# The address distance between the weight ring and the activation buffers in a two-layer decoder trunk

## What is computed

```python
h = x
for i in range(DEPTH):                      # DEPTH = 2
    xn = rmsnorm(h, g_mix[i])
    mix = attn_mixer(xn, ...) if i % 2 == 0 else rglru_mixer(xn, ...)
    h = h + mix
    h = h + swiglu(rmsnorm(h, g_ffn[i]), w_ffn_gate[i], w_ffn_up[i], w_ffn_down[i])
    gate = jax.nn.sigmoid(rmsnorm(h, g_ple[i]) @ w_ple_gate[i])
    h = h + gate * (p[i] @ w_ple_proj[i])   # p[i]: 256 tokens x 256
return rmsnorm(h, g_final)
```

## The kernel before

| tile | bytes from the ring's start | modulo 256 |
|---|---|---|
| w_hi, place s | 4224 s | 0, 128, 0, 128 |
| w_lo, place s | 16,896 + 4224 s | 0, 128, 0, 128 |
| pT_hi, pT_lo | 43,008 and 47,104 | 0 |
| xa_hi (a_off) | 56,640 | 64 |
| xa_lo, xb_hi, xb_lo, hid_hi | each 16,384 further | 64 |
| hid_lo | 45,056 behind hid_hi | 64 |

## Time and profile before

### The profile page before, as it was taken

How to read it: one execution, slowest core, us unless ns; L and a number is a source line. 1 busy time by engine, 2 the same in 40 slices (tenths; PEclk the granted TensorE clock), 3 DMA queues, 4 the chain that set the end, 5 groups by cost and what they waited for, 6 DMA issues and landing times.

```text
span 2471.5 us, 29756 instructions
## 1 busy us (share of the span) xinstructions
PE 2445.6 (99%) x11084; PEld 1994.7 (81%) x11084; DVE 1315.4 (53%) x1677; ACT 1139.5 (46%) x1533; POOL 3.2 (0%) x17
## 2 busy tenths in 40 slices
PE   8999999999999999999999999999999999999997
PEld 7888778888888888888888888888888888888886
DVE  5545665555454454444566676554454454444455
ACT  5435555544444444444454575544444444344454
POOL 0000000000000000000000000000000000000000
PEclk9999999999999999999999999999999999999999
DMA  7744435666666665555557445566666666555563
GB/s 215 229 120 120 131 117 182 185 187 186 187 187 182 186 186 184 187 188 187 187 187 235 140 154 178 186 183 185 187 187 184 186 183 188 186 187 187 187 204 135
DMA packets 234042, 443.87 MB, mean 180 GB/s; under 512 B 16184, under 2 KB 21344, under 8 KB 233824
## 3 DMA queue, kind: packets, MB, share of 16 engines
q1 hardware_dynamic: 233904, 442.62, 58.7%
q10 hardware_dynamic: 48, 0.02, 0.0%
HBM read 440.49 MB, written 2.10 MB: 179 GB/s over the span
## 4 chain that ended last, share of the span: by engine, by line
PE 96%; DVE 1%; ACT 1%; DMA 1%; issue 0%; ACTq 0%; DVEq 0%
PE ps L1278 30%; PE ps L1276 30%; PE ps L1277 30%; PE ps L1232 2%; PE ps L1487 1%; PE ps L1400 1%; PE ps L1331 1%; DMA raw<-in_w_in_rec_dram 1%; DVE w_lo L774 0%; ACT w_hi L537 0%; PE ps L1412 0%; PE ps L1437 0%; ACT prob L691 0%; DMA h<-in_x_dram 0%; PE ps L1371 0%
## 5 line engine op out<-in xcount | busy, mean ns | idle before, releaser
L774 DVE TENSOR_TENSOR w_lo<-raw,w_hi 128x1024 fp32r<-128x1024 f32 x820 | 998.4, 1220 | 1071.1 <-ACT w_hi L537 1070.1
L537 ACT ACTIVATE w_hi<-raw 128x1024 fp32r<-128x1024 f32 x820 | 863.1, 1055 | 1137.3 <-PE ps L1278 1108.2
L1278 PE MATMUL ps<-w_hi,xa_lo 128*128 128x512 f32 x1664 | 656.9, 395 | 0.0
L1277 PE MATMUL ps<-w_lo,xa_hi 128*128 128x512 f32 x1664 | 654.2, 393 | 0.0
L1276 PE MATMUL ps<-w_hi,xa_hi 128*128 128x512 f32 x1664 | 653.9, 393 | 0.0
L1277 PEld LDWEIGHTS ps<-w_lo,xa_hi 128*128 128x128 f32 x1664 | 312.7, 188 | 73.1
L1276 PEld LDWEIGHTS ps<-w_hi,xa_hi 128*128 128x128 f32 x1664 | 312.6, 188 | 70.5
L1278 PEld LDWEIGHTS ps<-w_hi,xa_lo 128*128 128x128 f32 x1664 | 312.6, 188 | 68.8
L1276 PE MATMUL ps<-w_hi,xb_hi 128*128 128x512 f32 x864 | 351.3, 407 | 3.9 <-DVE xb_lo L837 2.3
L1278 PE MATMUL ps<-w_hi,xb_lo 128*128 128x512 f32 x864 | 341.9, 396 | 0.0
L1277 PE MATMUL ps<-w_lo,xb_hi 128*128 128x512 f32 x864 | 341.0, 395 | 0.0
(11 more groups left out here) (200 smaller groups left out, 1043.9 us busy)
## 6 DMA issues: line engine op xcount, KB each, us to landing
raw<-in_w_ffn_gate_dram SPq DMA_DIRECT2D x176, 512.0 KB, 3.6
raw<-in_w_ffn_up_dram SPq DMA_DIRECT2D x176, 512.0 KB, 3.6
raw<-in_w_ffn_down_dram SPq DMA_DIRECT2D x176, 512.0 KB, 3.6
raw<-in_w_in_attn_dram SPq DMA_DIRECT2D x88, 512.0 KB, 3.7
raw<-in_w_ple_gate_dram SPq DMA_DIRECT2D x64, 512.0 KB, 3.8
raw<-in_w_in_rec_dram SPq DMA_DIRECT2D x64, 512.0 KB, 4.3
raw<-in_w_out_attn_dram SPq DMA_DIRECT2D x32, 512.0 KB, 3.7
raw<-in_w_out_rec_dram SPq DMA_DIRECT2D x32, 512.0 KB, 3.7
```

The costliest lines, as they stand in the source:

```text
L537: nc.scalar.activation(w_hi[:, s, 0:n], raw[:, s, 0:n], ACT.Copy).then_inc(hi_ready, 1)
L774: nc.vector.tensor_tensor(w_lo[:, s, 0:n], raw[:, s, 0:n], w_hi[:, s, 0:n].bitcast(F32), ALU.subtract).then_inc(lo_ready, 1)
L1277: nc.tensor.matmul(o, xh[:, k, tok], w_lo[:, s, wk], start=False, stop=False)
L1278: ins = nc.tensor.matmul(o, xl[:, k, tok], w_hi[:, s, wk], start=False, stop=(k == nkt - 1))
```

## The change

The ring slots of w_hi and w_lo lose their 32 elements of padding (4224 to 4096 bytes), and the offset of the large activation buffers is moved up by up to 255 bytes, until it agrees with the offset of w_hi modulo 256. No instruction, semaphore or transfer is added or removed.

```diff
-WROW = 2 * CW + 32
+PERIOD = 256
...
         raw = put("raw", [NRING, 2 * CW])
-        w_hi = put("w_hi", [NRING, WROW], F32R)
-        w_lo = put("w_lo", [NRING, WROW], F32R)
+        w_off = top[0]
+        w_hi = put("w_hi", [NRING, 2 * CW], F32R)
+        w_lo = put("w_lo", [NRING, 2 * CW], F32R)
...
-        a_off = top[0]
+        a_off = top[0] + (w_off - top[0]) % PERIOD
         big = a_off + 2 * KD * S * 4
         s_off = big + 2 * KD * S * 4
```

## The result

The changed kernel takes 2436.0 us (median of 4 runs, 2434.6 to 2436.5) against 2473.5 us of the kernel before on the same chip: ratio 0.985, 95% interval 0.983 to 0.986. The forecast was 2436. The profiled execution took 2436.5 us around a span of 2434.8.

What follows compares the result with a forecast made beforehand. TensorE's matmul count times start-to-start distance was taken as the bound; -40 us from aligned slots and +3 us lost gave -37, so 2473.3 - 37 = 2436 us, range 2428 to 2457, chance 0.62.

Steps and rivals of the forecast that it cites:

- What bounds the kernel: TensorE, busy 99% of the span: time is 9792 matmuls times their start-to-start distance, 9.8 us for each nanosecond.
- The control: Short PLE projections reading pT in ring places 0 and 2, already at distance 0: 226.4 ns a matmul, against 230.8 mean.
- Step (a): Ring without padding, alone: distance 192 everywhere, all slots at 2.79 us, 16 us more than before.
- Step (b): Activation buffers aligned to the ring: every large product at distance 0, a slot 2.720 us against 2.770, 40 us less.
- Rival 1: The uneven start comes in every slot, 2.745 us each: gain 20 us less 1 to 3, 2455 us; chance 0.18.
- step (e): Attention stage and its end: other engines' chains are late next, so 3 us of gain lost, ends 0 and 6.
- Rival 2: The ring slot's own place counts, not the distance: every slot 2.79 us, +16 us, 2490 us; chance 0.06.
- Rival 3: Change doesn't do what it says, or distance matters only for pT: 230.8 ns stays, 2473 us; chance 0.08.
- theory N: Follow-up forecast: only the running matmul's ring read and next weight load must agree; 2436 us with low parts moved 128 bytes.
- Rival 4: With all operands aligned the steady state shrinks to 224 ns or below: 23 us more gained, 2413 us; chance 0.06.
- (c): Some 128 small transposes and value products change distance with the moved area: bound about 1 us either way, taken as 0.
- (d): ScalarE's copy and VectorE's subtraction stay at 1055 and 1220 ns, hidden behind TensorE: nothing; wait for w_lo under 3 us.

Runs made afterwards that it cites:

- the circle of distances: Changed kernel, activation buffers moved further; ring minus activations modulo 256 of 32: 2493.7 us, 64: 2453.8, 96: 2493.7, 128: 2485.0, 224: 2493.4.

## Why the prediction was right, point by point

**What bounds the kernel.** Right: the whole gain is the distance between matmuls. 816 slots times 0.050 us are 40.8 us, and the spans differ by 36.7.

**The control.** The decisive step was to look for the same instruction at the distance that the change would give, in the trace before it. 48 matmuls out of 9792 had it, and their steady 226.4 ns stand against 226.7 measured. The run with all moved by 64 and the one moved by 256 bear out what the argument took from them, that the distance counts and not the place, and that its period is 256.

**Step (a), the ring alone.** +16 us forecast, +21 measured. The term was mis-sized because 2.79 us came from slow slots that follow a quick one. Among slow neighbours a slot takes 2.80.

**Step (b), the slot of 2.720 us.** Right to the last digit, but by two small errors that cancel. The steady distance is 0.3 ns longer than I took, and the first distance of a slot, 230 ns in the prediction, is not a cost of the wait on the ring: at distance 0 it is 226.7 ns on average like the others, while with distance 64 everywhere it is 231 ns. It belonged to the uneven pace of the other distances.

**Rival 1.** Its mechanism is real and was rightly kept out of most slots: the uneven start comes behind a slot of another distance, as the prediction argued, and the run with only the activations moved shows it there in slot after slot. It comes behind small matmuls as well, which the prediction hadn't named; that part remains in the changed kernel and is most of what step (e) lost in the attention stage.

**Rival 2.** The ring's own place is ruled out by the circle of distances: the ring stands where it does in the changed kernel, only the activations move, and the time goes from 2436 to 2494 us. **Rival 3** falls with the result, and the rule of the Trainium skill beside it (TensorE: Matmul & The Clock Gate, Part 2, step 1, that loading the next weights takes nothing from the running matmul) gave no change for any of these layouts. Between distance 0 and 32 lie 58 us with full loads, and there the measurement decides: the layout does change the time. Whether it is the load that takes read bandwidth from the running matmul no run shows: theory N, its plainest form, failed. **Rival 4** was not seen in any run; nothing was quicker than 2.72 us a slot.

**Steps (c) and (d).** No run separates (c), the small matmuls that changed distance. ScalarE and VectorE kept their means, and no wait of TensorE grew by more than 1 us: its longest after are 4.0 us for the first DMA, before 3.2, and 2.5 and 2.3 us as before. All waits of TensorE for w_lo together are 2.2 us (0.6 before), within the 3 us that the prediction allowed. These are the rows of its waits after:

```profile
PE ps L1495 <- DMA gmix<-in_g_mix_dram: 4.0, 1, 4.0
PE ps L1233 <- DVE xb_lo L838: 2.5, 1, 2.5
PE ps L1277 <- DVE xb_lo L838: 2.3, 1, 2.3
PE ps L1277 <- DVE w_lo L775: 1.6, 1, 1.6
...
PE ps L1267 <- DVE w_lo L775: 0.6, 1, 0.6
```

**Step (e), what eats the gain.** The prediction took 3 us, 4.1 were lost (40.8 - 36.7). That the sum is right to 1 us all the same is luck: it had rounded 40.8 down to 40, which makes up for most of it. Two stages can be read from the start of a slot before and after. Slot 124, the first behind the attention, and slots 424 and 460, before and in the recurrence, start in the kernel before at

```profile
458.83 0.39 PE L1276 MATMUL ps<-w_hi,xa_hi 128*128 128x512 f32 x1
...
1306.67 0.39 PE L1276 MATMUL ps<-w_hi,xb_hi 128*128 128x512 f32 x1
...
1425.50 0.48 PE L1276 MATMUL ps<-w_hi,xb_hi 128*128 128x512 f32 x1
```

and in the changed kernel at

```profile
454.71 0.39 PE L1277 MATMUL ps<-w_hi,xa_hi 128*128 128x512 f32 x1
...
1287.99 0.39 PE L1277 MATMUL ps<-w_hi,xb_hi 128*128 128x512 f32 x1
...
1406.12 0.47 PE L1277 MATMUL ps<-w_hi,xb_hi 128*128 128x512 f32 x1
```

The first 124 slots, 120 of them large, gained 4.1 us of 6.0, so 1.9 were lost there. Between slots 424 and 460 the lead grows from 18.7 to 19.4 us, 0.7 of 1.8, so 1.1 were lost in the recurrence, which the prediction had left out. The remaining 1.1 are spread over all other slots. The two losses have different causes in the traces. In the first stage no wait for w_lo came to a large slot; there matmuls that follow one another directly are 228.2 ns apart after and 231.2 before, a gain of 3.0 ns and not of 4.1 (226.8 and 230.9 in slots 124 to 424), because small matmuls lie between the slots and the pace has to settle again each time. In the recurrence it is one wait: at 1335.10 us TensorE waits 1.6 us for w_lo, where it waited 0.6 before. The distance of the two starts around that wait grew by 0.97 us, and TensorE, quicker, has begun to wait on the ring there. The stall at the attention's end stayed (2.3 us), with one stretch at the lower clock behind it, as in the kernel before.

## What to carry to other kernels

Where TensorE streams one buffer and loads weights from another at every matmul, look up the two offsets modulo 256 bytes: in this kernel, whose large matmuls are all 128x512 in fp32r, the same instructions ran between 2436 and 2494 us by this alone, and padding a ring changes the distance from place to place. Align both, and all parts of a split operand, and change the two together, since either half alone was worth 4 us or cost 21. To find such an effect, compare start-to-start distances of equal instructions by buffer place in the timeline, as TensorE's busy share is 99% before and after, and look in the same trace for a small group that already stands as the change would have it.

## What was not expected of the hardware

- The time jumps with the distance: 2436 us at 0, 2494 at 32 and at 224, 2454 at 64.
- On the way to distance 0, from another distance or from small matmuls in between, TensorE takes about four matmuls (0.93 us) to come to its even pace, and in other places of the attention stage up to ten. Alternating between 64 and 192 costs nothing.
- A weight load of 64 columns instead of 128, 134 ns instead of 188, came with a slower aligned kernel (2461 against 2436 us) and a quicker one at distance 32 (2470 against 2494).
- At the lower clock (1.2 GHz) the distance doesn't show. The first matmuls of each run, which are at that clock, start 0.43 us (426 to 427 ns) apart with each of the seven distances of the table; the effect is there at 2.4 GHz alone.
